# A fused two-layer decoder trunk on one core: a fifth seven-product pair in each gated layer's down projection

## The reference

```python
def swiglu(x, w1, w3, w2):
    return (jax.nn.silu(x @ w1) * (x @ w3)) @ w2     # w1, w3: 1024 x 2816; w2: 2816 x 1024
x = layer_norm(ALPHA * x + 0.5 * swiglu(x, ...), g, b)
```

## Time and profile before

| | |
|---|---|
| median of 3 runs | 1949.56 us (1949.47 to 1949.95) |
| profiled execution: span from first to last instruction | 1948.8 us |
| TensorE busy | 1928.0 us, 99% |
| VectorE, GpSimd, ScalarE busy | 1084.5, 898.8, 633.4 us |
| matmuls | 10793 |

### The profile page before, as it was taken

One profiled execution on the slowest core, in us unless ns is written; L12 is line 12 of the kernel. 1 busy time (PEld: TensorE's weight loads), 2 busy tenths in 40 slices (PEclk: granted clock), 3 DMA queues, 4 the chain that ended last, 5 costly groups with the idle time before them and its releaser, 6 DMA issues.

```text
span 1948.8 us, 26135 instructions
## 1 busy us (share of the span) xinstructions
PE 1928.0 (99%) x10793; PEld 1633.9 (84%) x10793; DVE 1084.5 (56%) x1620; ACT 633.4 (32%) x789; POOL 898.8 (46%) x596
## 2 busy tenths in 40 slices
PE   8999999999999999999999999999999999999997
PEld 8888888978788888888988888889988988888886
DVE  2755473555373665653465647265544675546655
ACT  3333232264423233322333323232233123323321
POOL 4453555533324455445445446444433345355544
PEclk9999999999999999999999999999999999999999
DMA  6232322321204333232423232322222222332321
GB/s 235 92 106 87 130 87 87 106 74 66 66 23 152 109 107 108 65 108 87 152 87 108 65 129 87 108 87 88 69 84 66 66 77 97 108 128 89 108 66 44
DMA packets 135590, 185.45 MB, mean 95 GB/s; under 512 B 3360, under 2 KB 119088, under 8 KB 135472
## 3 DMA queue, kind: packets, MB, share of 16 engines
q1 hardware_dynamic: 135312, 183.53, 28.5%
q10 hardware_dynamic: 160, 0.26, 0.1%
HBM read 181.42 MB, written 2.10 MB: 94 GB/s over the span
## 4 chain that ended last, share of the span: by engine, by line
PE 97%; DVE 2%; DMA 1%; ACT 0%; issue 0%; SPq 0%; POOL 0%; DVEq 0%; ACTq 0%
PE psum L1506 31%; PE psum L1507 30%; PE psum L1508 30%; PE psum L1816 2%; PE psum L1757 1%; PE psum L1530 1%; PE psum L1789 1%; PE psum L1770 1%; DMA raw<-in_ffn_w 1%; PE psum L1844 0%; PE psum L1847 0%; PE psum L1834 0%; DVE xt_lo L1015 0%; DVE arena L1212 0%; ACT w_hi L757 0%
## 5 line engine op out<-in xcount | busy, mean ns | idle before, releaser
L694 POOL TENSOR_TENSOR w_lo<-raw,w_hi 128x512 fp32r<-128x512 f32 x524 | 848.8, 1652 | 922.4 <-ACT w_hi L757 897.8
L1506 PE MATMUL psum<-xt_hi,w_hi 128*128 128x512 f32 (+1 forms) x1824 | 675.0, 370 | 2.2 <-DVE w_lo L1372 0.9
L1507 PE MATMUL psum<-xt_lo,w_hi 128*128 128x512 f32 (+1 forms) x1824 | 670.8, 368 | 0.0
L1508 PE MATMUL psum<-xt_hi,w_lo 128*128 128x512 f32 (+1 forms) x1824 | 670.7, 368 | 0.0
L1506 PEld LDWEIGHTS psum<-xt_hi,w_hi 128*128 128x128 f32 x1824 | 343.8, 188 | 65.3 <-issue 4.5
L1508 PEld LDWEIGHTS psum<-xt_hi,w_lo 128*128 128x128 f32 x1824 | 343.8, 189 | 57.1
L1507 PEld LDWEIGHTS psum<-xt_lo,w_hi 128*128 128x128 f32 x1824 | 343.9, 189 | 55.9
L757 ACT ACTIVATE w_hi<-raw 128x2048 fp32r<-128x2048 f32 x132 | 251.7, 1911 | 345.4 <-PE psum L1508 343.5
L1076 DVE SCALAR_TENSOR_TENSOR x<-psum,x 128x512 f32<-128x512 f32 x224 | 145.6, 684 | 131.5 <-PE psum L1508 128.3
L771 ACT ACTIVATE gate<-psum 128x512 f32<-128x512 f32 x88 | 52.5, 598 | 307.9 <-PE psum L1508 307.9
L1506 PE MATMUL psum<-w_hi,xt_hi 128*128 128x256 f32 (+2 forms) x448 | 139.8, 312 | 0.0
(11 more groups left out here) (178 smaller groups left out, 2147.1 us busy)
## 6 DMA issues: line engine op xcount, KB each, us to landing
raw<-in_ffn_w SPq DMA_DIRECT2D x115, 1024.0 KB, 5.4
raw_odd<-in_ffn_w SPq DMA_DIRECT2D x16, 1024.0 KB, 5.1
raw<-in_hgrn_w_in SPq DMA_DIRECT2D x16, 1024.0 KB, 5.5
raw<-in_attn_w_in SPq DMA_DIRECT2D x9, 1024.0 KB, 6.2
raw<-in_attn_w_out SPq DMA_DIRECT2D x4, 1024.0 KB, 4.9
raw<-in_hgrn_w_out SPq DMA_DIRECT2D x4, 1024.0 KB, 5.0
lng<-in_ln_g SPq DMA_DIRECT2D x6, 512.0 KB, 4.3
lnb<-in_ln_b SPq DMA_DIRECT2D x6, 512.0 KB, 5.4
```

Source lines behind the costliest of these rows:

```text
L694: op = pool.tensor_tensor(w_lo[:, slot_of[s], cols], raw[:, slot_of[s], cols], w_hi[:, slot_of[s], cols].bitcast(F32), ALU.subtract)
L1506: pe.matmul(out_, w[0], xs[0], start=first, stop=False)
L1507: pe.matmul(out_, w[0], xs[1], start=False, stop=False)
L1508: return pe.matmul(out_, w[1], xs[0], start=False, stop=last)
```

## The change

`NP` becomes 5, so groups 8 and 9 form a fifth pair (`LAST` = 4), and only group 10 is left to the direct way. The fifth pair does not look like the others:

- Its order on TensorE is: up w1 of group 10, P1, up w3 of group 10 block 0 alone, P6, P5, block 1, P7, and then `last_downs`.
- P4, P2 and P3 have no instruction of their own that adds them to x. They are the first matmuls of the PSUM accumulation that the down product of group 10 ends: P4 with the output's first half of token tiles 0 and 1; P2 and P3 with the two halves of tiles 2 and 3.
- B21 and B22 have buffers of their own (B22 over the right sums once these are used).
- The kept sums: VectorE adds kept1 to kept6 (`sum_kept`), then kept6 to three quarters of x (`bring_kept`) at three places in its queue; GpSimd adds kept1 to the fourth (`add_corner`).
- Token halves trade places in all pairs: the first block row now stands for tokens 256 to 511 (`left_source`, `x_piece`).
- The ring rotates differently from layer to layer, and the ring's spare buffer is free for the next phase once P4 of the fifth pair is done.

```diff
-NP = 4
-UPS = 2 * NG - 1
-FFN_RING = UPS + 4
+NP = 5
+LAST = NP - 1
+UPS = 2 * NG
+FFN_RING = UPS + 1
+LAST_PRODUCTS = ["P1", "P6", "P5", "P7", "P4"]
+LAST_RIGHT_HALF = {"B11": 0, "T2": 1, "T1": 0, "T3": 1, "T4": 0}
```

In `right_free`, what a right operand waits for before its high part is written:

```diff
+            if p == LAST:
+                return {"B21": (up1_done, 2 * (NG * f + 1) + 2),
+                        "B11": (product_done, product_count(f, p - 1, "P4")),
+                        "T2": (product_done, product_count(f, p - 1, "P3")),
+                        "T1": (product_done, product_count(f, p, "P1")),
+                        "T3": (product_done, product_count(f, p, "P6")),
+                        "T4": (product_done, product_count(f, p, "P5")),
+                        "B22": (right_lo_ready, right_count(f, p, "T3"))}[name]
```

ScalarE's queue after pair 3 (where lines are left out it makes the high parts of group 10's hidden features):

```diff
+                    left_high(fi, LAST, "A12")
+                    left_high(fi, LAST, "S1")
+                    right_high(n, fi, LAST, "B11")
+                    high(s0 + UPS - 1)
+                    for name in ("S2", "S3", "S4", "A22"):
+                        left_high(fi, LAST, name)
+                    gates(G0 + NG - 1)
+                    right_high(n, fi, LAST, "T2")
+                    right_high(n, fi, LAST, "T1")
+                    high(s0 + UPS)
+                    right_high(n, fi, LAST, "T3")
+                    right_high(n, fi, LAST, "T4")
...
+                    right_high(n, fi, LAST, "B22")
```

VectorE's queue after pair 3 (where lines are left out stand first the low parts of group 10's hidden features, then waits for its own and GpSimd's additions):

```diff
                     hiddens(G0 + NG - 2)
-                    add_product(fi, NP - 1, "P4", 4, [(1, 0)], weight)
-                    dve.wait_ge(product_added, N_ADDED * NP * (fi + 1))
-                    for k in range(8):
-                        add_piece(K0, k, weight, bank[4:8])
-                    hid_low(hid_odd, H0 + 1)
-                    hiddens(G0 + NG - 1)
+                    for name in ("S1", "S3", "S2"):
+                        left_sum(fi, LAST, name)
+                    left_low(fi, LAST, "A12")
+                    left_sum(fi, LAST, "S4")
+                    add_product(fi, LAST - 1, "P4", 4, [(1, 0)], weight)
+                    left_low(fi, LAST, "S1")
+                    right_low(n, fi, LAST, "B11")
+                    for name in ("S2", "S3", "S4", "A22"):
+                        left_low(fi, LAST, name)
+                    for name in RIGHT_SUMS:
+                        right_sum(n, fi, LAST, name)
+                    keep_product(fi, LAST, "P1", 4, kept1, weight)
+                    right_low(n, fi, LAST, "T2")
+                    right_low(n, fi, LAST, "T1")
+                    hiddens(G0 + NG - 1, (0,))
+                    keep_product(fi, LAST, "P6", 6, kept6, weight)
+                    sum_kept(fi)
+                    right_low(n, fi, LAST, "T3")
+                    add_product(fi, LAST, "P5", 4, [(0, 1), (1, 1)], weight)
+                    right_low(n, fi, LAST, "T4")
+                    bring_kept(1, 0)
+                    hiddens(G0 + NG - 1, (1,))
+                    bring_kept(1, 1)
...
+                    add_product(fi, LAST, "P7", 0, [(1, 0), (1, 1)], weight)
+                    bring_kept(0, 1)
+                    right_low(n, fi, LAST, "B22")
...
+                    last_down_and_norm(n, K0, weight)
```

TensorE's queue after pair 3:

```diff
-                    up(s0 + UPS - 1, G, up1_done, gate_done, 0)
-                    pe.wait_ge(product_added, N_ADDED * NP * (fi + 1))
-                    down(s0 + UPS, K0, H0)
-                    up(s0 + UPS + 1, G, up3_done, hid_done, 2)
-                    last_downs(n, s0 + UPS + 2, K0 + 1, H0 + 2)
+                    up(s0 + UPS - 2, G, up1_done, gate_done, 0)
+                    product(n, fi, LAST, "P1", 4)
+                    up(s0 + UPS - 1, G, up3_done, hid_done, 2, (0,))
+                    product(n, fi, LAST, "P6", 6)
+                    product(n, fi, LAST, "P5", 4)
+                    up(s0 + UPS - 1, G, up3_done, hid_done, 2, (1,))
+                    product(n, fi, LAST, "P7", 0)
+                    last_downs(n, fi, s0 + UPS, K0, H0)
```

The core of the new `last_downs`. `product_part` is 6 matmuls of a product, `down_part` 6 of group 10's down product. At t == 0, P4's part is followed by the waits for group 10's down slab and hidden features:

```diff
+                for t in (0, 1):
+                    product_part("P4", t, 0).then_inc(product_done, 1)
...
+                    down_part(t, 0, False)
+                    down_part(t, 1, True)
+                for t in (2, 3):
+                    product_part("P2", t, 0)
+                    down_part(t, 0, False)
+                    if t == 3 and n < last_phase:
+                        turn(n + 1, 1)
+                    product_part("P3", t, 1)
+                    down_part(t, 1, False)
+                    if t == 2 and n < last_phase:
+                        turn(n + 1, 0)
```

More of the change, by code:

```diff
@@ L80 @@
 N_ADDED = 18
+LAST_PRODUCTS = ["P1", "P6", "P5", "P7", "P4"]
+LAST_RIGHT_ORDER = ["B21", "B11", "T2", "T1", "T3", "T4", "B22"]
+LAST_RIGHT_HALF = {"B11": 0, "T2": 1, "T1": 0, "T3": 1, "T4": 0}
+LAST_ADDED = {"P1": 0, "P6": 2, "P5": 4, "P7": 8}
+PRODUCTS_OF_FFN = 14 * LAST + 2 * len(LAST_PRODUCTS)
+ADDED_OF_FFN = N_ADDED * LAST + 12
 def layout(phases):
@@ L491, in left_source, with right_parts @@
                     "S3": hid[:, :, second], "S4": hid_odd[:, :, first]}[name]
-        def right_parts(n, name):
-            cols = slice(RIGHT_HALF[name] * SLAB // 2, (RIGHT_HALF[name] + 1) * SLAB // 2)
+        def right_parts(n, p, name):
+            if p == LAST and name == "B21":
+                return b21_hi[:], b21_lo[:]
+            if p == LAST and name == "B22":
+                return b22_hi[:], b22_lo[:]
+            half = (LAST_RIGHT_HALF if p == LAST else RIGHT_HALF)[name]
+            cols = slice(half * SLAB // 2, (half + 1) * SLAB // 2)
             return [part[:, spare_slot[n], cols].rearrange("p (c n) -> p c n", c=2) for part in (w_hi, w_lo)]
@@ L710, in shift, with add_corner @@
                     pool.tensor_tensor(x[:, t, :], x[:, t, :], lnb[:], ALU.add).then_inc(ln_done, 1)
+            def add_corner(f):
+                pool.wait_ge(product_added, added_count(f, LAST, "P1", 2))
+                for t in range(2):
+                    part = x[:, 2 + t, 0:HALF]
+                    pool.tensor_tensor(part, part, kept1[:, t, :], ALU.add).then_inc(corner_added, 1)
             pool.wait_ge(lo_ready, 2)
@@ L922, in _ @@
                     right_high(n, fi, 0, "B21")
-                    for p in range(NP):
+                    for p in range(LAST):
                         if p == 0:
@@ L1064, in x_piece @@
             def x_piece(row, t, half):
[L1066 removed]
+                return x[:, 2 * (1 - row) + t, half * HALF:(half + 1) * HALF]
             def add_product(f, p, name, b0, targets, weight):
@@ L1532, in turn, with up @@
                     mm.then_inc(turn_done, 1)
-            def up(s, G, done, freed, b0):
+            def up(s, G, done, freed, b0, blocks=(0, 1)):
                 pe.wait_ge(lo_ready, s + 1)
-                for j in range(2):
+                for j in blocks:
                     pe.wait_ge(freed, 2 * G - 1 + j)
```

184 lines of the change are left out of this document (80 added, 104 removed).

## The result

The changed kernel takes **1968.52 us** (median of 4 executions, 1967.72 to 1972.67), against 1949.65 for the kernel before on the same chip (4 executions). The ratio is 1.0101, 95% interval 1.0089 to 1.0113: one per cent slower, 12.9 us above the forecast of 1955.6 and outside its range. The profiled execution took 1972.67 and its span is 1970.9, 22.1 above the span before; the spans of the other three are 1966.0 to 1967.3.

The account below looks back on a forecast made before the run. TensorE, busy 99% of the span, was taken as the bound. From the profiled 1948.8: -11.0 (matmuls) + 15.0 (slab waits) + 2.1 (layer ends) = 1954.9; the median lies 0.8 above the span, so 1955.6, range 1953 to 1957.

Parts of the forecast that it names:

- Matmuls: On TensorE: 12 matmuls fewer per gated layer, 48 in all, at 0.229 us each, a gain of 11.0 us.
- The slab for up w3: Fifth pair, group 10: GpSimd's low half of this slab comes late, so TensorE waits 3.74 us per layer after P1.
- T2's one turn: Fifth pair: VectorE's low part of T2 goes before GpSimd's fourth slab instruction, raising TensorE's wait from 2.75 to 3.74 us.
- no hold: Rival at the fifth pair's slab: T2 does not delay GpSimd's fourth instruction; wait 2.75 us, total 1949.6 to 1951.7; chance 0.15.
- two turns: Rival at the fifth pair's slab: T1's low part also precedes GpSimd's fourth instruction; 4.6 us more, 1960.2; chance 0.09.
- full gain: Rival at the fifth pair's slab: its low half is ready by +2.6, no wait appears; 1938.6 us; chance 0.08.
- Hidden features: Group 10, before the first down part: VectorE's low parts end at 26.2, needed at 27.0; no wait, margin under 1 us.
- The end of the layer: Before the next phase's transposes: tile 0 is 0.55 us late; 0.7 us with tile 1, in three layers, 2.1 in all.
- Tile 1's normalising: At the layer's end: GpSimd's second slab of the next phase makes tile 1 about 0.15 us late.
- The clock: TensorE's granted clock in the fifth pair's gap of about 3.6 us: forecast to stay full, so nothing was charged.
- two signs of being wrong: In the profile after: granted clock leaving 1.00 in the fifth pair; other waits of a microsecond behind the slab's wait.
- The rival: Granted clock falls in the fifth pair's gap, block 0's 24 matmuls take up to twice as long; 1966 us; chance 0.09.

## Why the prediction was wrong

- **Matmuls: right.** 48 fewer at 0.229 us are 11.0. With the waits removed (P6 first, GpSimd's additions, tile 1) the kernel takes 1941.94, and 4 x 0.42 of known wait are in it: 1940.3 without, which is 9.6 under before. Of the remaining 1.4 of the 11.0, 0.6 is in the windows of the run with P6 first: P1 takes 2.81 us and P6 2.84 instead of 2.75 each, in four layers. The rest I did not trace.
- **The slab for up w3: right in mechanism, 0.38 us too large in size.** 3.36 instead of 3.74 per layer, and 0.14 more in block 0 behind the gap, which the prediction did not have; TensorE starts 0.05 us after GpSimd's end and not 0.36. T2's one turn is worth 0.99, and T1 goes behind GpSimd, as argued. The rivals "no hold", "two turns" and "full gain" did not happen.
- **Hidden features: right for this kernel.** No wait before the first down part; without the two large gaps 0.4 us shows.
- **The end of the layer: wrong, the larger miss.** The step that failed is "there GpSimd has just started the next phase's first slab and holds the port 0.6 us". The low part of a slab is four instructions in a row, and each of VectorE's next three with two SBUF inputs waited for one of them: 2.6 us. I had counted the hold that was under way and not the queue behind it. Tile 1's normalising was taken at one turn, 0.15, and meets GpSimd in both its instructions. Turn 0 is 2.55 late and 0.89 remains behind it at full clock (8.35 us to the next phase with the gaps filled, 7.46 before), instead of 0.7 together: 8.2 us in three layers.
- **The clock: wrong.** The step is "The gap here is shorter, so I take no fall". The one fall in the trace before, 4.1 us after the last matmul of all, was taken as a bound for a gap; the clock fell behind each of seven gaps of 2.4 to 3.4 us. That costs 5.3 us on the medians. The prediction had named two signs of being wrong that came true: the clock leaves 1.00 in the fifth pair, and other waits of over a microsecond stand behind the slab's. The rival said 1966 and had 0.09. That its number comes near 1968.5 is luck: it had the fall right, but at 10.8 us in the four up projections, about twice what the clock cost in all, and the rest came from the end of the layer. In the Trainium skill, TensorE: Matmul & The Clock Gate, section "Why this matters for your kernels", the rule against idle gaps names this loss, and the filled gaps agree with it: 5.3 us came back. Not every gap brings it here, though: 21 of 28 did.

On the medians: -1.0 (slab, 4 x (0.14 - 0.38)) + 8.2 + 5.3 = 12.5 of the 12.9 missed; 0.4 stays open. The same matmuls in another order of the queues, with two additions and one wait more on GpSimd, gain 0.4%; as the change orders them they lose 1.0%.

## What to carry to other kernels

When two engines take turns at a shared resource, count how many instructions each has ready in a row at that place: every one of mine that follows may wait for one of theirs, not only the first. A gap that a reordering opens on TensorE costs its own length, and it can cost slow matmuls behind it, here 0.8 or 1.6 us behind three gaps in four; price both, or put a product there that needs nothing late. And when one queue's order is changed, ask for each moved item what its operands stand behind in the other queues: P6 moved alone gained 5.9 us (1959.35 to 1953.44), with VectorE's and ScalarE's order 16.0.

## What the runs showed of the hardware

- The granted clock fell from 2.4 to 1.2 GHz behind gaps of 2.4 us (window 326 to 327 of the run in which VectorE waits for the slab), although after the program's last matmul it stayed full for 4.1 us. Six traces here have TensorE gaps of 2.1 to 3.2 us as the lists of waits give them, 28 in all: the clock fell behind 21 (7 of 7 in the changed kernel, 4 of 7 with T2 behind the slab, 3 of 4 with the additions on GpSimd, 3 of 3 and 2 of 3 at the turn in two others, 2 of 4 in front of P6), 7 of the 8 of 3.2 us and 14 of the 20 shorter ones. It can fall after TensorE has started again: in the changed kernel's third layer block 0 starts at 1261.59, the next microsecond has 0.99, the one after it 0.50. So the time since TensorE stopped is not by itself what decides; what does was not settled.
- Matmuls whose result nobody reads kept the clock full through all seven waits, and the kernel gained 5.3 us by them.
- VectorE and GpSimd can hand the port to and fro for many instructions, each taking its own time plus the rest of the other's (1.74, 1.78, 1.75, 2.32, 2.27 in the rows above), while an instruction of VectorE with one operand in PSUM beside a running one of GpSimd stays at 0.69. They do not always alternate: GpSimd's instruction at 313.52 waited 8.11 us through a run of VectorE's. No run settles which of the two happens.
